# Projection weights as one contiguous run per partition and load; the table of bias by distance written 16 times and read in 8 pieces

## The reference

```
xn = rmsnorm(h, ln_mix_g[l])
proj = xn @ w_in[l]
nsa_q, nsa_kv, nsa_gate, c_q, c_kv, k_rope, merge_gate = split_cols(proj, IN_SPLITS)
o_nsa = nsa_mixer(...)      # compressed, selected and window branch, bias by distance
o_mla = mla_mixer(...)      # low rank queries and keys, rotary part
merged = gates[:, :, 0] * (o_nsa @ w_branch_nsa[l]) + gates[:, :, 1] * (o_mla @ w_branch_mla[l])
h = h + merged @ w_out[l]
h = h + peer_ffn(rmsnorm(h, ln_ffn_g[l]), ...)   # 128 x 128 experts, top 16 per head
```

## Time and profile before

| | us |
|---|---|
| runs before | 1292.7, 1294.8, 1296.26 (median 1294.8) |
| profiled execution, span | 1292.7 |
| TensorE busy (matmul) | 1125.5 (87%) |
| VectorE busy | 841.7 (65%) |
| GpSimd busy | 771.3 (60%) |
| ScalarE busy | 530.8 (41%) |
| 16 DMA engines, queue of SyncE | 40.2% of their time, 170.99 MB |
| 16 DMA engines, queue of GpSimd | 1.4% of their time, 3.15 MB |

### The profile page before, as it was taken

One profiled execution on the slowest core, in us unless ns is written; L12 is line 12 of the kernel. 1 busy time (PEld: TensorE's weight loads), 2 busy tenths in 40 slices (PEclk: granted clock), 3 DMA queues, 4 the chain that ended last, 5 costly groups with the idle time before them and its releaser, 6 DMA issues.

```text
span 1292.7 us, 22881 instructions
## 1 busy us (share of the span) xinstructions
PE 1125.5 (87%) x7526; PEld 963.3 (75%) x7526; DVE 841.7 (65%) x1136; ACT 530.8 (41%) x1057; POOL 771.3 (60%) x519
## 2 busy tenths in 40 slices
PE   7399999999999989888888887778778778899997
PEld 6166888848999989888888886556556556788885
DVE  1014333220899930699999998999999999544443
ACT  2025324222767767433333333333233233455554
POOL 0000000001799998788888877666566566799996
PEclk9698999999999999989899988888888788999999
DMA  9763231311355545433434343333332232456553
GB/s 295 186 235 131 77 93 44 131 39 59 114 165 176 163 162 178 135 129 127 130 114 143 116 130 108 106 127 98 97 130 97 97 130 97 148 194 194 189 189 125
DMA packets 59556, 174.52 MB, mean 135 GB/s; under 512 B 5007, under 2 KB 19504, under 8 KB 59528
## 3 DMA queue, kind: packets, MB, share of 16 engines
q1 hardware_dynamic: 58408, 170.99, 40.2%
q0 software_dynamic: 1120, 3.15, 1.4%
HBM read 171.50 MB, written 2.62 MB: 135 GB/s over the span
## 4 chain that ended last, share of the span: by engine, by line
issue 35%; PE 31%; DVE 23%; POOL 7%; DVEq 2%; ACT 1%; DMA 0%; POOLq 0%; ACTq 0%
PE ps L962 31%; DVE B L893 10%; POOL lo L392 7%; DVE A L888 6%; DVE marks L889 5%; DVE wl L907 1%; ACT wh L593 0%; DVE big L901 0%; PE ps L965 0%; DMA x_early<-x 0%; DVEq L907 0%; DVEq L893 0%; DVEq L901 0%; ACT big L638 0%; DVEq L937 0%
## 5 line engine op out<-in xcount | busy, mean ns | idle before, releaser
L392 POOL TENSOR_TENSOR lo<-raw,hi 128x512 fp32r<-128x512 f32 x512 | 768.4, 1516 | 461.3 <-ACT hi L562 449.4
L562 ACT CAST hi<-raw 128x512 fp32r<-128x512 f32 x512 | 317.5, 621 | 510.4 <-PE ps L962 509.1
L962 PE MATMUL ps<-xh,hi 128*128 128x256 f32 x1024 | 300.6, 294 | 11.5 <-POOL lo L392 9.5
L962 PE MATMUL ps<-xl,hi 128*128 128x256 f32 x1024 | 295.4, 288 | 0.0
L962 PE MATMUL ps<-xh,lo 128*128 128x256 f32 x1024 | 294.7, 288 | 0.0
L962 PE MATMUL ps<-hi,wh 128*128 128x512 f32 x512 | 218.2, 426 | 64.5 <-DVE wl L907 64.5
L893 DVE TENSOR_TENSOR B<-marks,g_part 128x512 bf16<-128x512 bf16 x192 | 245.7, 1332 | 7.5
L962 PEld LDWEIGHTS ps<-xh,hi 128*128 128x128 f32 x1024 | 203.0, 198 | 14.2 <-POOL lo L392 12.8
L962 PE MATMUL ps<-lo,wh 128*128 128x512 f32 x512 | 211.1, 412 | 0.0
L962 PE MATMUL ps<-hi,wl 128*128 128x512 f32 x512 | 211.0, 412 | 0.0
L962 PEld LDWEIGHTS ps<-xl,hi 128*128 128x128 f32 x1024 | 202.8, 198 | 0.0
(11 more groups left out here) (191 smaller groups left out, 880.6 us busy)
## 6 DMA issues: line engine op xcount, KB each, us to landing
raw<-u_t SPq DMA_DIRECT2D x128, 512.0 KB, 3.5
raw<-v_t SPq DMA_DIRECT2D x128, 512.0 KB, 3.5
big<-w_in SPq DMA_DIRECT2D x10, 1024.0 KB, 5.7
area<-w_out SPq DMA_DIRECT2D x1, 4096.0 KB, 13.2
big<-w_query SPq DMA_DIRECT2D x1, 4096.0 KB, 12.8
big<-w_in SPq DMA_DIRECT2D x1, 2784.0 KB, 44.9
big<-w_in SPq DMA_DIRECT2D x1, 2048.0 KB, 18.6
area<-w1k SPq DMA_DIRECT2D x1, 2048.0 KB, 50.9
```

Source lines behind the costliest of these rows:

```text
L392: nc.gpsimd.tensor_tensor(lo[:, b:b + KH * P], raw[:, a:a + KH * P], as_f32(hi[:, b:b + KH * P]), ALU.subtract).then_inc(lo_ready, 1)
L562: nc.scalar.copy(hi[:, b:b + KH * P], raw[:, a:a + KH * P]).then_inc(hi_ready, 1)
L962: return nc.tensor.matmul(o, lhsT, rhs, start=start, stop=stop, **kw)
```

## The change

On the host each matrix is laid out anew. A piece of columns becomes an array of 128 rows, one per partition, in which the 8 runs of that partition follow each other, and the pieces stand side by side in memory. Each load then copies one contiguous run per partition: 8 KB for the first two pieces of `w_in`, 16 KB for the third, 22,272 bytes for the fourth, 8 KB for a merge chunk, 32 KB for both compression weights in one load, 10 KB for both low rank weights in one, 32 KB for both branch weights in one, and 32 KB for `w_out` and for `w_query`. Bytes and order stay as they are. In SBUF the tile `win` is split into four, one behind the other, and a small function finds the one that holds given columns.

The table in memory becomes [8, 16, 383]: each head is written 16 times instead of 128. It is read back by eight transfers of 16 partitions, each with a start shifted by 16. `bias_in` now counts to 128.

```
+SHEAR = 16
+PIECES = ((0, K0 // 2), (K0 // 2, K0), (K0, REST0), (REST0, PART_A))
...
-        win = part(big, 0, KT, PART_A)
+        wins = [part(big, KT * a, KT, b - a) for a, b in PIECES]
+
+        def win(k, a, b):
+
+            lo_, w_ = next(((x0, w_) for (x0, x1), w_ in zip(PIECES, wins) if x0 <= a and b <= x1))
+            return w_[:, k, a - lo_:b - lo_]
...
+        wu = part(big, 22016, 2 * H * QK + H * 2 * DH)
...
-        rev_dram = nc.dram_tensor("bias_by_distance", [H, P, DIST], fp32, kind="Internal")
+        rev_dram = nc.dram_tensor("bias_by_distance", [H, SHEAR, DIST], fp32, kind="Internal")
...
-            for n, (a, b) in enumerate(((0, K0 // 2), (K0 // 2, K0), (K0, REST0), (REST0, PART_A))):
-                sp.dma_start(win[:, :, a:b], w_in_t[:, :, a:b]).then_inc(win_in[n], 16)
-            sp.dma_start(w1[:, 0], w1k.rearrange("(k p) c -> p k c", p=P)).then_inc(w1_in, 16)
-            sp.dma_start(w1[:, 1], w1v.rearrange("(k p) c -> p k c", p=P)).then_inc(w1_in, 16)
-
-            sp.dma_start(wuq, w_uq.rearrange("(k p) c -> p k c", p=P)).then_inc(wu_in, 16)
-            sp.dma_start(wukv, w_ukv).then_inc(wu_in, 16)
+            for n, (a, b) in enumerate(PIECES):
+                sp.dma_start(big[:, KT * a:KT * b], w_in[:, KT * a:KT * b]).then_inc(win_in[n], 16)
+            sp.dma_start(area[:, :], w_1).then_inc(w1_in, 16)
+            sp.dma_start(wu, w_u).then_inc(wu_in, 16)
...
-                lo = MERGE0 + c * 256
-                sp.dma_start(mslot[c % 2], w_in_t[:, :, lo:lo + 256]).then_inc(merge_in[c % 2], 16)
+                a, b = KT * (MERGE0 + c * 256), MG + c % 2 * KT * 256
+                sp.dma_start(big[:, b:b + KT * 256], w_in[:, a:a + KT * 256]).then_inc(merge_in[c % 2], 16)
...
-            sp.dma_start(wb[:, 0], w_bn.rearrange("(k p) c -> p k c", p=P)).then_inc(wb_in, 16)
-            sp.dma_start(wb[:, 1], w_bm.rearrange("(k p) c -> p k c", p=P)).then_inc(wb_in, 16)
+            sp.dma_start(big[:, 0:2 * 4 * D], w_b).then_inc(wb_in, 16)
...
-            sp.dma_start(wo, w_out.rearrange("(k p) c -> p k c", p=P)).then_inc(wo_in, 16)
+            sp.dma_start(area[:, :], w_out).then_inc(wo_in, 16)
...
-            sp.dma_start(wq, w_query.rearrange("(k p) c -> p k c", p=P)).then_inc(wq_in, 16)
+            sp.dma_start(big[:, MG:MG + KT * D], w_query).then_inc(wq_in, 16)
...
-            pool.dma_start(rev_dram.ap(), spread(revS, P)).then_inc(rev_out, 16)
+            pool.dma_start(rev_dram.ap(), spread(revS, SHEAR)).then_inc(rev_out, 16)
             pool.wait_ge(rev_out, 16)
-            pool.dma_start(biasM, bass.AP(rev_dram, P - 1, [[DIST - 1, P], [P * DIST, H], [1, T]])).then_inc(bias_in, 16)
+            for r in range(0, P, SHEAR):
+                pool.dma_start(biasM[r:r + SHEAR], bass.AP(rev_dram, P - 1 - r, [[DIST - 1, SHEAR], [SHEAR * DIST, H], [1, T]])).then_inc(bias_in, 16)
```

More of the change, by code:

```diff
@@ L56, with build @@
 KH = KT // 2
-def build(nc, x, g_fin, w_in, w1k, w1v, w_uq, w_ukv,
-          w_bn, w_bm, w_out, w_query, keys_t, u_t, v_t, t5, one_hot, keep_pack, early_pack, out):
+SHEAR = 16
+PIECES = ((0, K0 // 2), (K0 // 2, K0), (K0, REST0), (REST0, PART_A))
+def build(nc, x, g_fin, w_in, w_1, w_u, w_b, w_out, w_query, keys_t, u_t, v_t, t5, one_hot, keep_pack, early_pack, out):
     fp32, u32 = mybir.dt.float32, mybir.dt.uint32
@@ L316, in _ @@
         def _(sp):
-            w_in_t = w_in.rearrange("(k p) c -> p k c", p=P)
             for i in range(NT):
@@ L742, in _ @@
                               bcast(hmaskS[0:H * NC, :], DH), ALU.mult).then_inc(vb_ready, 1)
-            dve.wait_ge(bias_in, 16)
+            dve.wait_ge(bias_in, 16 * (P // SHEAR))
             dve.wait_ge(gate_ready, 1)
@@ L999, in job @@
                         r = 2 * n + j
-                        last = project(b[:, j * T:(j + 1) * T], lambda k: win[:, k, r * P:(r + 1) * P],
+                        last = project(b[:, j * T:(j + 1) * T], lambda k: win(k, r * P, (r + 1) * P),
                                        turn=0 if r == 0 else None)
@@ L1005, in job @@
                         c = K0 + j * P
-                        last = project(b[:, j * T:(j + 1) * T], lambda k: win[:, k, c:c + P])
+                        last = project(b[:, j * T:(j + 1) * T], lambda k: win(k, c, c + P))
                 elif n == J_CK:
@@ L1009, in job @@
                         c = CK0 + kv * P
-                        last = project(b[:, kv * T:(kv + 1) * T], lambda k: win[:, k, c:c + P])
+                        last = project(b[:, kv * T:(kv + 1) * T], lambda k: win(k, c, c + P))
                 elif n == J_V:
@@ L1013, in job @@
                         for k in range(KT):
-                            last = mm(b[:, i * T:(i + 1) * T], xnT3[:, k, i * P:(i + 1) * P], win[:, k, V0:REST0],
+                            last = mm(b[:, i * T:(i + 1) * T], xnT3[:, k, i * P:(i + 1) * P], win(k, V0, REST0),
                                       start=k == 0, stop=k == KT - 1)
@@ L1019, in job @@
                     for k in range(KT):
-                        last = mm(b[:, 0:REST], xnT3[:, k, i * P:(i + 1) * P], win[:, k, REST0:CK0],
+                        last = mm(b[:, 0:REST], xnT3[:, k, i * P:(i + 1) * P], win(k, REST0, CK0),
                                   start=k == 0, stop=k == KT - 1)
@@ L1033, in job @@
                 elif n < J_VM:
-                    pe.wait_ge(wu_in, 32)
+                    pe.wait_ge(wu_in, 16)
                     wait_job_evacuated(pe, J_CR)
@@ L1062, in _ @@
                 job(n)
-            pe.wait_ge(w1_in, 32)
+            pe.wait_ge(w1_in, 16)
             pe.wait_ge(job_dve, 1)
@@ L1179, in _ @@
             pe.wait_ge(oT_ready, 4)
-            pe.wait_ge(wb_in, 32)
+            pe.wait_ge(wb_in, 16)
             for c in range(KT):
@@ L1348 @@
         w[:, end:end + REST], kv[:, 0].reshape(D, P), kv[:, 1].reshape(D, P), w[:, end + REST:]], axis=1)
+    flat = lambda z: z.reshape(-1, P, z.shape[-1]).transpose(1, 0, 2).reshape(P, -1)
+    pieces = PIECES + tuple((MERGE0 + n * 256, MERGE0 + (n + 1) * 256) for n in range(8))
+    w_in = np.concatenate([flat(w_in[:, p0:p1]) for p0, p1 in pieces], axis=1)
+    both = lambda y, z: np.concatenate([flat(a[y][0]), flat(a[z][0])], axis=1)
     w2k = a["nsa_cmp_k_w2"][0]
@@ L1356 @@
         "w_in": w_in,
-        "w1k": a["nsa_cmp_k_w1"][0], "w1v": a["nsa_cmp_v_w1"][0],
-        "w_uq": a["mla_w_uq"][0], "w_ukv": a["mla_w_ukv"][0],
-        "w_bn": a["w_branch_nsa"][0], "w_bm": a["w_branch_mla"][0], "w_out": a["w_out"][0],
-        "w_query": a["peer_w_query"][0],
+        "w_1": both("nsa_cmp_k_w1", "nsa_cmp_v_w1"), "w_u": both("mla_w_uq", "mla_w_ukv"),
+        "w_b": both("w_branch_nsa", "w_branch_mla"), "w_out": flat(a["w_out"][0]),
+        "w_query": flat(a["peer_w_query"][0]),
         "keys_t": a["peer_sub_keys"][0].transpose(1, 3, 0, 2).reshape(P, H, NK),
```

## The result

| | before | after | ratio, 95% interval |
|---|---|---|---|
| first comparison, median us (4 runs each) | 1293.75 (1292.0 to 1296.26) | 1275.18 (1272.29 to 1275.87) | 0.9843 [0.9815, 0.9871] |
| second, 11 and 6 runs | 1293.62 | 1278.33 | 0.9864 [0.9821, 0.9907] |
| third, 10 and 6 runs | 1296.16 | 1277.10 | 0.9849 [0.9819, 0.9879] |
| profiled execution, span | 1292.7 | 1274.0 | |

What follows compares the result with a forecast made beforehand. TensorE's 20.0 us wait for the fourth piece of `w_in`, held back by the bias table's write, bounds the start. 1292.7 - 19.98 (stall) - 2.96 (clock) = 1269.8 us as profiled, so a median of 1272, range 1267 to 1275.

Steps and rivals of the forecast that it cites:

- The time: Median of the whole changed kernel: 1272 us, own range 1267 to 1275; chance of the forecast 0.62.
- the one up to 1283: Wider range of the median, up to rival A's full price, given a chance of over 0.8.
- rival A: DMA engines, 20 to 40 us: new reads take 11.4 us, `w_in` late, TensorE stands 8.1 us; 1283 us; chance 0.25.
- The stall: TensorE's wait for the fourth piece of `w_in` from 32.86 us vanishes: minus 19.98 us.
- The clock: Matmuls after the stall, 5.92 us at 1.2 GHz, run at full clock: minus 2.96 us.
- The landing of the fourth piece: Last piece of `w_in` lands at 28.9 us: 23.7 + 0.5 + 2.5 + 2.2, at 412 GB/s.
- Eight reads: Reading the table back in eight transfers costs SyncE's queue 2.5 us of all engines, by bytes.
- Low end for the reads: Choice of 2.5 us by bytes as the reads' price for SyncE's queue, against a far end of 11.4 us.
- Rivals B and C: Long runs slow. B: 213 GB/s, 1290 us, chance 0.06. C: below 173 GB/s, slower than before, chance 0.04.
- The signs: No `w_in` wait, 32 wide matmuls 11.8 us, write 5 to 7 us, about 400 GB/s to 40 us, compression about 60.
- Later stages move as a whole: From the compression to the end the time stays the same within 3 us.
- The sum: 1292.7 - 19.98 - 2.96 = 1269.8 us for the profiled execution, 2.1 us under the median, so 1272.

Runs made afterwards that it cites:

- bias_only: Kernel before with only the table change (16 copies, eight reads), weights in the old layout; 1275.48 us, ratio 0.9859.
- runs_4k: Changed kernel with `w_in`, compression and low rank weights in chunks of 2.5 to 4 KB, 32 bytes of padding between them in memory; 1275.58 us, ratio 0.9825.
- weights_only: Kernel before with only the new weight layout, the table still written 128 times and read back once; 1275.23 us, ratio 0.9871.
- reads_idle: Changed kernel with the table's eight reads held back until no other transfer is under way; 1274.20 us (one run).

## Why the prediction was right, and by how much it was off

- **The time.** 1272 us forecast; 1275.18, 1278.33 and 1277.10 measured in the three comparisons. All lie above the forecast's own range of 1267 to 1275 and inside the one up to 1283, whose upper part was there for rival A. Rival A's wait did not come, so that the wider range holds is not to its credit: what filled it was the clock.
- **The stall.** The bound was named rightly, and it went to nothing, as forecast. Its size was off: 19.98 us was true of one execution. Over four profiles it is 16.8 us, and what moved is the start of J_R0, by 16.1 us (52.12 to 36.02 in the means). This is the term that was mis-sized: "the stall is gone, with 4 us to spare: minus 19.98 us" took for granted that TensorE wants the piece at 32.86. When it wants it depends on when the clock comes up at the start, 33 to 37 us, and only the stall had made that invisible.
- **The clock.** 2.96 us forecast, 2.96 in the profiled pair, 2.7 in the means (14.68 to 11.98).
- **The landing of the fourth piece.** 28.9 us forecast, 25.4 measured. The rate was 430 GB/s between 14 and 20 us instead of 412, and the table's 3 us of bytes mostly did not go first: the reads had not been issued yet.
- **Eight reads.** I priced them at their bytes, 2.5 us; alone they take 1.05 MB at 134 GB/s, 7.8 us, three times that. The mechanism of rival A is real: two thirds of its price alone, and an estimated 9 of its 11.4 us beside the short packets of bias_only, where TensorE waited 3.2 us for it. Low end for the reads was the wrong choice. It stayed off the path for a reason that the prediction did not have: the reads wait for the write, the write took 10.9 us among the long packets instead of the 5 to 7 forecast, and so the first read was issued at 25.11 with the fourth piece landing at 25.4. That was luck, though runs_4k, where they were issued from 20.7 on, had no stall either.
- **Rivals B and C.** Long runs are not slow: in the changed kernel the stream ran at 430 GB/s before the reads came in.
- **The signs.** There was no wait for `w_in`, and the 32 wide matmuls took 11.98 us (11.8 forecast). Three signs failed: the write took 10.9 us instead of 5 to 7, the transfers moved 206 to 237 GB/s at 36 to 40 us instead of 400, and the compression started at 63.07 instead of about 60.
- **Later stages move as a whole.** Not quite: from the compression to `xl` the changed kernel is 2.4 us longer in the means, all of it in the stretch at 1.2 GHz. The dip that the range allowed for ("may come or go, some 3 us") came. From `xl` to the end both kernels scatter between 996 and 1002 us.
- **The sum.** In means of all profiles: 18.8 us by the start of the compression, less 2.4 us up to `xl`, less 0.9 us behind it, 15.5 us in the spans (1292.0 to 1276.4), where 22.9 were forecast. In the two profiles whose clock ran as in the profile read (weights_only and reads_idle, 33.3 and 210.2 in the table) the start on `xl` came 22.6 and 22.5 us earlier: the sum is right for that case. One step of the arithmetic mixed two measures: the 2.1 us between the profile and the median set a span against a time. In every run that is listed with its span the time is 1.5 to 1.6 us longer in kernels with the old layout of the weights, and 1.7 to 2.0 with the new one. So the profiled execution took some 1294.3 us and stood only 0.5 us under the median. The result is the same, since 1294.8 less 22.9 is 1271.9; but some 0.3 us of what the spans gain is lost outside them.

## What to carry to other kernels

A stall measures a difference of two arrivals. Before its length is booked as gain, look for what happens inside it: here the engine that waited would itself have come about 3 us later than the profile read showed in three of four executions of the kernel before and in all three of the changed one. And where two queues share the transfer engines, count packets and not only bytes: a transfer from or to few partitions was slow here where its packets followed each other closely, and how much it held up a stream depended on how long the stream's packets were. Of two remedies that each remove the same stall, neither's gain adds to the other's.

## What the runs showed of the hardware that I had not expected

- Copies of the table on 8 partitions went at 46 GB/s when the engines with them had little else to do, and the stream waited for them; beside packets of 8 to 32 KB the same 1.57 MB took 42.9 us, ran at 25 GB/s per engine in what turns it got between 14 and 30 us, and cost the fourth piece nothing.
- Eight reads onto 16 partitions each slowed the other queue's packets as well: 10.6 GB/s per engine in bias_only between 24 and 36 us, instead of 21.8.
- Packets of whole runs, 26 KB on average, carry more than 4 KB ones: 430 GB/s between 14 and 20 us, and 404 in the same stretch of runs_4k.
- The granted clock of TensorE at the start of a launch is not shown by the windows (1.00 throughout) and yet differs: the same 96 matmuls took 20.99 to 23.19 us. The weight loads show it, 0.34 us instead of 0.19.
- Stretches at 1.2 GHz behind the compression are 6.8, 10.2, 13.6 or 20.5 us long in kernels that do the same work there, and nine matmuls in the gaps did not end one sooner.
